# A low part from GpSimd to VectorE, one step earlier and one later, at the end of a gated FFN's unit loop

## The reference

```python
D_MODEL, SEQ, DEPTH, D_FF, PLE_DIM = 2048, 256, 2, 5632, 256

def conv_gated_ffn(x, w_up, conv_w, conv_b, w_down):
    gu = x @ w_up
    gate, up = gu[..., :D_FF], gu[..., D_FF:]
    gate = causal_depthwise_conv(gate, conv_w, conv_b)
    return (jax.nn.silu(gate) * up) @ w_down

    for i in range(DEPTH):
        ...
        h = h + jnp.concatenate([y_pool, y_att], axis=-1) @ w_out[i]
        h = h + conv_gated_ffn(rms_norm(h, norm_ffn_g[i]), w_up[i], conv_w[i], conv_b[i], w_down[i])
        gate = jax.nn.sigmoid(rms_norm(h, norm_ple_g[i]) @ w_ple_gate[i])
        h = h + (p[i] @ w_ple[i]) * gate
    return rms_norm(h, final_norm_g)
```

## Time and profile before

| | us |
|---|---|
| median of three runs (2165.25 to 2165.63) | 2165.45 |
| the profiled execution | 2165.72 |
| its span, first to last instruction | 2163.9 |
| TensorE busy in it | 2145.5 (99%) |
| VectorE busy | 1707.7 (79%) |
| ScalarE busy | 1125.2 (52%) |
| GpSimd busy | 49.7 (2%) |

### The profile page before, as it was taken

How to read it: one execution, slowest core, us unless ns; L and a number is a source line. 1 busy time by engine, 2 the same in 40 slices (tenths; PEclk the granted TensorE clock), 3 DMA queues, 4 the chain that set the end, 5 groups by cost and what they waited for, 6 DMA issues and landing times.

```text
span 2163.9 us, 32717 instructions
## 1 busy us (share of the span) xinstructions
PE 2145.5 (99%) x11526; PEld 1861.5 (86%) x11526; DVE 1707.7 (79%) x2192; ACT 1125.2 (52%) x1422; POOL 49.7 (2%) x114
## 2 busy tenths in 40 slices
PE   9999999999999999999999999999999999999998
PEld 8898888888888888887898988888888888888786
DVE  5797569888889888896557875688888889888964
ACT  6556445554555554555554664545544545554554
POOL 2000000000000000000000000000000000000011
PEclk9999999999999999999999999999999999999999
DMA  8645555546655546655556455565546565546562
GB/s 267 212 139 175 176 200 196 175 163 224 213 194 195 175 164 222 213 175 189 178 181 183 137 175 176 204 208 177 183 166 233 201 207 182 179 164 233 175 214 97
DMA packets 233323, 406.75 MB, mean 188 GB/s; under 512 B 14828, under 2 KB 50268, under 8 KB 233096
## 3 DMA queue, kind: packets, MB, share of 16 engines
q1 hardware_dynamic: 231976, 402.72, 55.4%
q0 software_dynamic: 512, 1.76, 0.2%
q10 hardware_dynamic: 736, 1.07, 0.1%
HBM read 403.42 MB, written 2.10 MB: 187 GB/s over the span
## 4 chain that ended last, share of the span: by engine, by line
PE 95%; DVE 3%; issue 1%; ACT 1%; POOL 0%; POOLq 0%; DVEq 0%; ACTq 0%
PE acc L2079 16%; PE tps L2079 16%; PE acc L1898 11%; PE acc L1900 11%; PE acc L1899 11%; PE tps L2089 9%; PE acc L2089 8%; PE tps L1899 3%; PE tps L1900 3%; PE tps L1898 3%; PE tps L1955 1%; PE acc L1985 1%; DVE h L1536 1%; DVE w_lo L1566 1%; DVE xb_lo L1193 0%
## 5 line engine op out<-in xcount | busy, mean ns | idle before, releaser
L996 ACT ACTIVATE w_hi<-raw 128x1024 fp32r<-128x1024 f32 x540 | 559.2, 1058 | 536.4 <-PE acc L2089 116.6
L1566 DVE TENSOR_TENSOR w_lo<-raw,w_hi 128x1024 fp32r<-128x1024 f32 x540 | 650.0, 1226 | 165.8 <-ACT w_hi L996 152.4
L1181 DVE TENSOR_TENSOR w_lo<-raw,w_hi 128x1024 fp32r<-128x1024 f32 (+1 forms) x288 | 342.2, 1211 | 143.7 <-ACT w_hi L722 138.1
L722 ACT ACTIVATE w_hi<-raw 128x1024 fp32r<-128x1024 f32 (+2 forms) x287 | 290.1, 1044 | 179.1 <-PE acc L1900 126.4
L2079 PE MATMUL acc<-xa,w_hi 128*128 128x512 f32 x1536 | 366.1, 391 | 0.0
L2079 PE MATMUL tps<-xa,w_hi 128*128 128x512 f32 x1536 | 361.2, 390 | 0.0
L2079 PEld LDWEIGHTS tps<-xa,w_hi 128*128 128x128 f32 x1536 | 285.4, 188 | 57.1
L2079 PEld LDWEIGHTS acc<-xa,w_hi 128*128 128x128 f32 x1536 | 283.8, 188 | 56.1 <-DVE h L1521 0.4
L1899 PE MATMUL acc<-w_hi,xb_lo 128*128 128x512 f32 x640 | 249.2, 389 | 0.0
L1898 PE MATMUL acc<-w_hi,xb_hi 128*128 128x512 f32 x560 | 220.7, 394 | 1.0 <-ACT pw L1072 1.0
L1900 PE MATMUL acc<-w_lo,xb_hi 128*128 128x512 f32 x560 | 218.3, 390 | 0.0
(11 more groups left out here) (262 smaller groups left out, 2656.4 us busy)
## 6 DMA issues: line engine op xcount, KB each, us to landing
raw<-in_w_up SPq DMA_DIRECT2D x176, 1024.0 KB, 5.0
raw<-in_w_down SPq DMA_DIRECT2D x88, 1024.0 KB, 5.0
raw<-in_w_out SPq DMA_DIRECT2D x32, 1024.0 KB, 5.1
raw<-in_w_ple_gate SPq DMA_DIRECT2D x32, 1024.0 KB, 5.0
raw<-in_w_in SPq DMA_DIRECT2D x21, 1024.0 KB, 5.3
raw<-in_w_ukv SPq DMA_DIRECT2D x8, 1024.0 KB, 5.4
raw<-in_w_in SPq DMA_DIRECT2D x8, 864.0 KB, 4.8
raw<-in_w_uq SPq DMA_DIRECT2D x6, 1024.0 KB, 5.5
```

The source lines that it names most:

```text
L722: copy(w_hi[:, half_of(m), 0:n], raw[:, c % RAW_SLOTS, at:at + n], ACT.Copy).then_inc(hi_done, 1)
L996: copy(w_hi[:, half_of(m), :], raw[:, c % RAW_SLOTS, half * HALF:(half + 1) * HALF], ACT.Copy).then_inc(hi_done, 1)
L1181: dve.tensor_tensor(w_lo[:, half_of(m), 0:n], raw[:, c % RAW_SLOTS, at:at + n], w_hi[:, half_of(m), 0:n].bitcast(F32), ALU.subtract).then_ ...
L1566: dve.tensor_tensor(w_lo[:, half_of(m), :], raw[:, slot, half * HALF:(half + 1) * HALF], w_hi[:, half_of(m), :].bitcast(F32), ALU.subtract ...
```

## The change

Three edits. (1) On GpSimd the wait and the subtraction that make the low part of the last gated tile are gone; VectorE makes it instead, by its helper `lo`, as the first thing behind the loop. The semaphore `g_lo` that TensorE waits for is raised there. (2) In each unit of the loop VectorE's two adds of the last plain block stand between the last two low splits, where they stood behind both. (3) In the tail TensorE transposes the third block of `h` (j = 3) behind the second half of block 3, where it did so between its halves; the transposes of the first two blocks stay.

```diff
@@ GpSimd, each layer
-                pool.wait_ge(g_hi, UNITS * l + UNITS)
-                pool.tensor_tensor(xa[1][:, 0:4, :], conv[:, :, :], xa[0][:, 0:4, :].bitcast(F32),
-                                   ALU.subtract).then_inc(g_lo, 1)
@@ VectorE, unit
-                    go(25, 27)
+                    go(25, 26)
                     for t in range(TT):
                         product_added(PLAIN_1 + 1, h_block(t, 1), tps[:, (3 + t) % T_BANKS, :], t, t_done,
                                       1 if t == 0 else 4)
+                    go(26, 27)
 
                 first_unit()
                 with dve.Fori(0, LOOPS) as w:
                     for i in range(TURN_UNITS):
                         unit(w, i)
+
+                dve.wait_ge(g_hi, UNITS * l + UNITS)
+                lo(xa[1][:, 0:4, :], conv[:, :, :], xa[0][:, 0:4, :]).then_inc(g_lo, 1)
@@ TensorE, tail
-                        elif i == 0:
+                        elif i == (1 if j == N_BLK - 1 else 0):
                             pe.wait_ge(h_ready, 3 * N_BLK * l + N_BLK + N_BLK + j)
                             turn_h(l, JB["ple_norm"], 2 * j - 2)
                             turn_h(l, JB["ple_norm"], 2 * j - 1)
```

## The result

The change makes the kernel slower: 2176.36 us, median of five runs (2175.84 to 2176.69), against 2165.31 us for the kernel before beside it (2165.10 to 2165.63). The ratio is 1.005 with a 95% interval of 1.0039 to 1.0062: +11.05 us where +9.6 was forecast (2175.1 us, range 2171.2 to 2177.5). The profiled execution took 2176.68 us with a span of 2174.9, 11.0 more than before, and a mean granted clock of 0.995 instead of 0.998.

What follows compares the result with a forecast made beforehand. TensorE, busy 99% of the span, bounds the kernel; only its tail waits move the time. Per layer 4.06 - 0.74 + 1.60 = 4.92, two layers 9.84, less 0.20: +9.6 on 2165.45, 2175.1 us, range 2171.2 to 2177.5.

Steps and rivals of the forecast that it cites:

- Part 1, the stall: Tail's first matmul: TensorE waits for the low part behind VectorE's adds and a split, 4.06 us a layer later.
- piece (b): VectorE's queue at the loop's end: the low split formerly ahead of the adds comes after them, 1.13 us of the stall.
- Part 1, the shared port: Loop's end: without GpSimd's operation VectorE's first split loses its 0.90 us slowdown and ends before the adds, costing nothing.
- Part 2: Loop's end: earlier adds free the PSUM bank before the transposes of p, -0.74 us a layer; 0 at the loop's 20 borders.
- Part 3: Tail: the third block's 2.17 us wait moves to the second bank pair, about 2.7 us; gain 0, first layer -0.20.
- Part 4, the clock: Behind the new stall in each layer's tail the granted clock falls, costing 1.60 us a layer, bounds 0 and 3.
- (B): Rival: clock stays up behind one or both new stalls, 2173.5 or 2171.9 us; chance 0.34 together.
- (C): Rival: moving the third block's transposes pays in full, second bank pair free before 2054.8, 2167.6 to 2169.2 us; chance 0.07.
- (D): Rival: low part done before TensorE asks at the loop's end, so faster, 2159.5 us, or 2163.8; chance 0.02.
- (E): Rival: the loop's new border costs TensorE 2 us, or low-clock stretches last twice as long, 2177 to 2179 us; chance 0.07.

Runs made afterwards that it cites:

- the run with the low part one place ahead: Changed kernel with each unit's last low split made first in the next unit, so the low part precedes it behind the loop: 2171.21 us, ratio 1.0030.
- part 2 alone: Kernel before with only the adds of the last plain block moved ahead of the last low split in every unit: 2163.87 us, ratio 0.9993.
- the filled one: Changed kernel with 16 unread matmuls of 512 columns in each layer ahead of TensorE's wait for the low part: 2172.13 us, ratio 1.0031.
- part 3 alone: Kernel before with only the third block's transposes one half later: 2165.54 us, ratio 1.0001.
- the reordered tail: Changed kernel with GpSimd keeping the low part, and VectorE's fourth-block adds right behind the third block's corner sums: 2156.09 us, ratio 0.9958.
- part 1 alone: Kernel before with only the low part of the last gated tile moved from GpSimd to VectorE behind the loop: 2174.33 us, ratio 1.0039.
- all parts in the better tail: Changed kernel plus VectorE's fourth-block adds behind the third block's corner sums and ScalarE's first copy ahead of the squares: 2168.39 us, ratio 1.0011.
- parts 2 and 3: Changed kernel without part 1, GpSimd keeping the low part: 2163.93 us, ratio 0.9993 against the kernel before.
- the better tail without part 3: The reordered tail with the third block's transposes again between the fourth block's halves: 2162.54 us, ratio 0.9987 against the kernel before.
- the fastest kernel: The reordered tail with ScalarE also copying the first products with p out of PSUM ahead of the fourth block's squares: 2155.49 us, ratio 0.9955.

## Why the prediction was right, point by point

- **Part 1, the stall (4.06 us a layer).** Right. The wait is 3.77 us and TensorE goes on 3.77 + 0.16 = 3.93 us late, by the chain that was forecast. The pick-up after the release was 0.05 us, not 0.14. That a piece of the queue counts in full was shown by the run with the low part one place ahead (-1.14 us). But the split in this sum, piece (b), is there by part 2 and not by part 1: without part 2 the stall was 3.46 us, and the 0.74 us were saved all the same. The forecast had the total of the two parts right and divided it wrongly between them.
- **Part 1, the shared port.** Right that it is worth nothing here: the first split fell from 2.13 to 1.21 us and the adds then idled 0.21 us for TensorE.
- **Part 2 (-0.74 a layer, 0 in the loop).** Right for part 2 alone, -1.5 us, and right for the loop. Beside part 1 it is no gain, as said above.
- **Part 3 (0 in the second layer, -0.20 in the first).** Right in its main point; the wait moved and was 2.5 us, where 2.7 was forecast. Missed by a little: I counted 0 for a low clock behind the moved wait. It came in both layers and cost 0.06 + 0.20 in the first and 0.25 in the second, 0.5 in all, within the bound of 0.5 a layer.
- **Part 4, the clock (+1.60 a layer).** Right that it comes in both layers. Its size was short in one: 4.92 us of shift in the second layer is just the forecast, though made of 3.93 - 0.74 + 1.73, and 6.04 in the first is 3.93 - 0.74 + 2.85. The price taken from the first layer's stall before (1.60) was one sample of something that varies: 2.85 and 1.73 here, of which some 0.1 us is the slower restart that the forecast had counted in the stall. This term is too small by 1.4 us and part 3's by 0.5; the stall came out 0.3 us shorter and the loop's end 0.36 us earlier, which leaves the 1.3 us between 2175.1 and 2176.36. That the sum came out so near owes something to these errors of opposite sign. The Trainium skill (TensorE: Matmul & The Clock Gate, "What's actually happening") says that the throttled state is the default and activity releases it. Both new stalls, with the clock at 0.50 behind them, and the filled one, with 1.00, agree; why a stall of 2.2 to 2.6 us lowers the clock in one layer and not in the other, no run here shows.
- **The rivals.** (B), the clock up behind one or both, was not seen in the changed kernel's five runs, which lie within 0.9 us. (C), part 3 in full, is refuted by part 3 alone, and its condition, the second bank pair free in time, is shown to be the right one by the reordered tail. (D) needed the low part done before TensorE asks for it, which no run with the low part on VectorE has. (E) has nothing in the loop for it; its other condition, longer low stretches, came in part, in the first layer, where the price was 2.85 us instead of 1.60.

## What to carry to other kernels

Work that is moved to an engine with time to spare costs by its place in that engine's queue: here 1.2 us of work stood behind an add that had to wait for TensorE, and TensorE waited for both. Removing a wait of the bounding engine is a gain only if the next thing it needs is ready earlier too, so follow the queue that releases it to the next release before moving the waiter. Cut the queue first: the same move of the transposes was worth 0 before VectorE's adds were brought forward and at least 4.4 us after.

## What the runs showed of the hardware

A stall of TensorE can cost twice, and the second cost differs between layers and executions of one program. In the profiled executions, counting the two layers of each: stalls of 3.5 to 3.8 us (the changed kernel, part 1 alone, all parts in the better tail) were followed by a low granted clock six times of six; those of 2.5 to 2.6 us (the changed kernel, part 3 alone, parts 2 and 3, the filled one, the low part ahead) eight times of twelve; those of 2.2 us (the kernel before, part 1 alone, part 2 alone, the better tail without part 3) once in eight.

Where the matmuls behind the stall were on the path, the price came in two sizes. It is read from the way between the tail's first matmul and the transposes of the first block, which is 8.81 us after the filled stall, with the clock up (965.02 - 956.21 in its first layer, 2042.23 - 2033.42 in its second). In three cases (the changed kernel's first layer, both layers of all parts in the better tail) the granted clock had already fallen in the last microsecond of the stall, to 0.57, 0.53 and 0.50, and the price was 2.5 to 2.75 us. In four (the changed kernel's second layer, both of part 1 alone, the first with the low part ahead) it fell only after TensorE had resumed, and the price was 1.5 to 1.6 us. Where a later wait took it up, it was a few tenths: the way to the first gate product was 26.87 us instead of 26.58 in the kernel before.

The widest scatter belongs to kernels whose matmuls behind a stall are on the path: 5.7 us over six runs with stalls of 2.6, 4.0 over eleven with stalls of 2.2 in the reordered tail, against 0.6 us over five in the fastest kernel, which has none in its tails. It is not a rule: the changed kernel itself, with its stalls of 3.8 us, stayed within 0.9 us. A single profile therefore does not give the price of a stall of 2 to 3 us.
